# Fourier mixers: transform x times the norm's weights over channels, the token's factor at the copy out of PSUM; x in four transfers at launch

## The reference

```python
def rms_norm(x, g):
    xf = x.astype(jnp.float32)
    y = xf * lax.rsqrt(jnp.mean(xf * xf, axis=-1, keepdims=True) + EPS)
    return (y * g.astype(jnp.float32)).astype(x.dtype)

def fourier_mixer(h, w_out):
    b, s, d = h.shape
    hg = h.astype(jnp.float32).reshape(b, s, N_FOURIER_GROUPS, FOURIER_GROUP)
    f = jnp.fft.fft2(hg, axes=(1, 3), norm="ortho").real
    return f.reshape(b, s, d).astype(h.dtype) @ w_out
```

## Time and profile before

| | |
|---|---|
| runs, median (lowest to highest) | 2574.54 us (2573.38 to 2581.89), 3 runs |
| profiled execution, first to last instruction | 2575.1 us; no other time of this execution is given |
| mean granted clock of TensorE | 0.981 of full speed |
| busy: TensorE, DVE, ACT, GpSimd | 96%, 69%, 49%, 9% |
| launch to the first projection | 34.5 us |
| end of the ffn before the second Fourier mixer to its projection | 21.5 us |

### The profile page before, as it was taken

How to read it: one execution, slowest core, us unless ns; L and a number is a source line. 1 busy time by engine, 2 the same in 40 slices (tenths; PEclk the granted TensorE clock), 3 DMA queues, 4 the chain that set the end, 5 groups by cost and what they waited for, 6 DMA issues and landing times.

```text
span 2575.1 us, 54629 instructions
## 1 busy us (share of the span) xinstructions
PE 2467.8 (96%) x23198; PEld 2410.2 (94%) x23198; DVE 1778.5 (69%) x2300; ACT 1260.1 (49%) x1508; POOL 220.8 (9%) x246
## 2 busy tenths in 40 slices
PE   7999779999999899999999999999999999999998
PEld 7999669999999889989999999999999998999998
DVE  5998956665555666657666669976667667986665
ACT  5444535335666553344344346565334335675433
POOL 5000140003000100000000000600000000330000
PEclk9999879999999899999999999999999999999999
DMA  5553024555676735535545544434555554434453
GB/s 216 181 200 122 19 84 177 190 191 190 172 179 175 171 121 193 194 139 180 195 179 196 195 173 150 150 135 165 196 195 180 196 195 147 157 141 150 186 191 127
DMA packets 65839, 430.76 MB, mean 167 GB/s; under 512 B 8288, under 2 KB 11360, under 8 KB 15904
## 3 DMA queue, kind: packets, MB, share of 16 engines
q1 hardware_dynamic: 58864, 410.30, 44.0%
q0 software_dynamic: 6000, 17.46, 4.5%
q10 hardware_dynamic: 832, 0.92, 0.1%
HBM read 426.45 MB, written 1.15 MB: 166 GB/s over the span
## 4 chain that ended last, share of the span: by engine, by line
PE 85%; DVE 8%; ACT 4%; issue 2%; DMA 0%; DVEq 0%; ACTq 0%
PE psum L2018 26%; PE psum L2019 25%; PE psum L2020 25%; DVE w_lo L1332 2%; ACT w_hi L847 1%; PE psum L2063 1%; PE psum L2228 1%; PE psum L2134 1%; PE psum L2377 1%; PE psum L2365 1%; DVE h L1351 1%; DVE h_lo L1340 1%; PE psum L2355 1%; PE psum L2321 0%; PE psum L2117 0%
## 5 line engine op out<-in xcount | busy, mean ns | idle before, releaser
L2018 PE MATMUL psum<-h_hi,w_hi 128*128 128x256 f32 x4320 | 1212.7, 281 | 16.8 <-DVE h_lo L1376 9.6
L2019 PE MATMUL psum<-h_lo,w_hi 128*128 128x256 f32 x4320 | 1202.4, 278 | 0.0
L2020 PE MATMUL psum<-h_hi,w_lo 128*128 128x256 f32 x4320 | 1202.0, 278 | 0.0
L1332 DVE TENSOR_TENSOR w_lo<-raw,w_hi 128x2048 fp32r<-128x2048 f32 x387 | 888.3, 2296 | 377.7 <-ACT w_hi L847 377.5
L847 ACT ACTIVATE w_hi<-raw 128x2048 fp32r<-128x2048 f32 x387 | 741.5, 1917 | 819.9 <-PE psum L2020 819.8
L2018 PEld LDWEIGHTS psum<-h_hi,w_hi 128*128 128x128 f32 x4320 | 817.0, 189 | 26.1 <-issue 19.1
L2019 PEld LDWEIGHTS psum<-h_lo,w_hi 128*128 128x128 f32 x4320 | 816.9, 189 | 0.5 <-issue 0.5
L2020 PEld LDWEIGHTS psum<-h_hi,w_lo 128*128 128x128 f32 x4320 | 816.4, 189 | 0.0
L2018 PE MATMUL psum<-act_hi,w_hi 128*128 128x256 f32 x1536 | 425.4, 277 | 0.7 <-DVE act_lo L1895 0.7
L2020 PE MATMUL psum<-act_hi,w_lo 128*128 128x256 f32 x1536 | 424.4, 276 | 0.0
L2019 PE MATMUL psum<-act_lo,w_hi 128*128 128x256 f32 x1536 | 424.4, 276 | 0.0
(11 more groups left out here) (334 smaller groups left out, 2359.6 us busy)
## 6 DMA issues: line engine op xcount, KB each, us to landing
raw<-in_panels SPq DMA_DIRECT2D x387, 1024.0 KB, 4.8
arena<-bias_by_distance POOLq DMA_DIRECT2D x32, 384.0 KB, 6.2
x<-in_x SPq DMA_DIRECT2D x1, 1024.0 KB, 5.7
arena<-in_s_cbd POOLq DMA_DIRECT2D x4, 256.0 KB, 2.9
arena<-in_s_b SPq DMA_DIRECT2D x1, 1024.0 KB, 15.2
arena<-in_s_c SPq DMA_DIRECT2D x1, 1024.0 KB, 17.1
hidden<-in_s_cbd POOLq DMA_DIRECT2D x4, 256.0 KB, 2.9
arena<-arena POOLq DMA_DIRECT2D x32, 32.0 KB, 1.9
```

The lines of the kernel that those rows point to most:

```text
L1332: v.tensor_tensor(w_lo[:, s, :], raw[:, s, :], w_hi[:, s, :].bitcast(F32), ALU.subtract).then_inc(lo_ready, 1)
L2018: t.matmul(o, w[0], xin[0], start=start, stop=False, skip_group_check=True)
L2019: t.matmul(o, w[0], xin[1], start=False, stop=False, skip_group_check=True)
L2020: return t.matmul(o, w[1], xin[0], start=False, stop=stop, skip_group_check=True)
```

## The change

- The norm ahead of a Fourier mixer no longer makes h = x * gain * rstd. DVE multiplies x by the gain alone (`gained`), for the second mixer between its additions at the end of the ffn before. C works on that.
- The token's factor is applied by ACT as the scale of the copy of C into `dft_tok`. As tokens are on the partitions there, the factor is a column: ACT's squares go to `dft_sums` (the memory of `hidden`), TensorE multiplies each 128x128 of them with one column of ones (`sums`, 32 passes instead of 16 of 256 columns), ACT takes the root of 128x2 and DVE its reciprocal. The copy is two instructions, one for each half of the tokens. The Sqrt table is loaded ahead of the squares.
- On TensorE the order is C(0), sums of the first three pairs, C(1), the last sums, T(0).
- At launch, x comes in four transfers with a semaphore each. gains and s5.par are issued by ACT, ahead of the DFT constants. The Exp comes before the first norm. The one-hot product, its mask, and the splits of panels 0 and 1 move into the first mixer's loop, S5's reciprocal behind it. ACT splits panel 2 before S5's trigonometry and not after.
- `load_dft` for the second mixer is issued at the start of the ffn before it.

The diff, cut: left out are declarations, counts of `const_loaded` that follow from the moves, and the loops over the stages from which the launch work is taken.

```diff
@@ -318,6 +321,7 @@
         DFT_O = S // 2 - 1
         dft_ch = arena[:, 0:2 * DFT_C]
         dft_sq = arena[:, S:S + 2 * (DFT_E + 2 * DFT_O)].rearrange("p (t n) -> p t n", t=2)
+        dft_sums = hidden[:, :, :, :, :].rearrange("p a b t s -> p (a b t) s")
         dft_tok = arena[:, 5 * S:5 * S + 2 * 2 * S].rearrange("p (b t n) -> p b t n", b=2, t=2)
@@ -579,10 +583,10 @@
 
         @block.sync
         def _(sp):
-            sp.dma_start(x[:, :, :], A["x"].rearrange("(c p) t -> p c t", p=P)).then_inc(x_loaded, 16)
-            sp.dma_start(gains[:, :], A["gains"]).then_inc(const_loaded, 16)
+            for b in range(4):
+                sp.dma_start(x[:, 2 * b:2 * b + 2, :], A["x"].rearrange("(c p) t -> p c t", p=P)[:, 2 * b:2 * b + 2, :]
+                             ).then_inc(x_loaded[b], 16)
             sp.dma_start(ident[:, :], A["ident"]).then_inc(const_loaded, 16)
-            sp.dma_start(s5.par, A["s5_lam"].rearrange("p (r c) -> p r c", r=3)).then_inc(const_loaded, 16)
             for n in range(SLOTS):
                 sp.dma_start(raw[:, n, :], A["panels"][n]).then_inc(panel_loaded[n], 16)
             for dst, name in ((s5.b, "s5_b"), (s5.c, "s5_c")):
@@ -850,11 +854,27 @@
                 a.dma_start(dft_ch, A["dft_ch"]).then_inc(dft_loaded, 16)
                 a.dma_start(dft_sq, A["dft_sq"].rearrange("(t p) n -> p t n", p=P)).then_inc(dft_loaded, 16)
 
+            def squares_of_columns(st):
+
+                n = st["norm"]
+                a.wait_ge(const_set, 4)
+                a.activation(warm[:, :], eps[:, :], ACT.Sqrt)
+                for b in range(4):
+                    if st["xr"]:
+                        a.wait_ge(x_ready, st["xr"] - 3 + b)
+                    else:
+                        a.wait_ge(x_loaded[b], 16)
+                    a.activation(dft_sums[:, 2 * b:2 * b + 2], x[:, 2 * b:2 * b + 2, :], ACT.Square).then_inc(sq_ready, 1)
+                a.wait_ge(ss_ready, n + 1)
+                a.activation(rcol[:, :], bank[3][:, 0:2], ACT.Sqrt, bias=eps[:, 0:1], scale=1.0 / D).then_inc(rms_ready, 1)
+
             def norm(st):
                 n = st["norm"]
-                a.wait_ge(x_loaded, 16)
+                if st["dft"]:
+                    squares_of_columns(st)
+                    return
                 if st["late"]:
-                    a.wait_ge(const_loaded, 48)
+                    a.wait_ge(gains_loaded, 16)
                     if st["after_ffn"]:
                         a.wait_ge(panel_done, st["n0"] - 1)
                     for b in range(4):
@@ -871,8 +891,6 @@
                                  ACT.Square).then_inc(sq_ready, 1)
                 if st["late"]:
                     split(st["n0"] + 2)
-                if st["dft"] and st["xr"]:
-                    load_dft()
                 a.wait_ge(const_set, 4)
 
                 a.activation(warm[:, :], eps[:, :], ACT.Sqrt)
@@ -904,6 +922,8 @@
                         a.wait_ge(act_ready, f * FFC + c + 1 if i is None else i * 2 + f * FFC + c + 1)
                         a.activation(act_hi[:, c % 2], act[:, c % 2], ACT.Copy).then_inc(act_hi_ready, 1)
 
+                if st["next_dft"]:
+                    load_dft()
                 split(n0 + 3)
                 silu(0, n0)
                 high(0)
@@ -930,19 +950,25 @@
                     a.wait_ge(dft_full, f * KT + 2 * b + 2)
                     a.activation(h_hi[:, 2 * b:2 * b + 2], h[:, 2 * b:2 * b + 2], ACT.Copy).then_inc(dft_hi_ready, 1)
 
+                a.wait_ge(rstd_ready, st["hn"] + 1)
                 for g in range(KT):
                     a.wait_ge(dft_tok_ready, f * KT + g + 1)
-                    a.activation(dft_tok[:, g % 2, :, 0:2 * DFT_C], bank[4 + g % 2][:, :].rearrange(
-                        "p (t n) -> p t n", t=2)[:, :, 0:2 * DFT_C], ACT.Copy).then_inc(dft_tok_copied, 1)
+                    for m in range(2):
+                        ins = a.activation(dft_tok[:, g % 2, m, 0:2 * DFT_C], bank[4 + g % 2][:, m * S:m * S + 2 * DFT_C],
+                                           ACT.Copy, scale=rcol[:, m:m + 1])
+                    ins.then_inc(dft_tok_copied, 1)
                     if g:
                         even(g - 1)
                     if g >= 3 and g % 2:
                         high((g - 3) // 2)
+                    if f == 0 and g in (2, 5):
+                        split(g // 3)
                 even(KT - 1)
                 high(KT // 2 - 1)
+                split(st["n0"] + 2)
                 if f == 0 and any(q["kind"] == "s5" for q in stages):
                     s5_prepare()
-                for p in range(4):
+                for p in range(1, 4):
                     split(st["n0"] + p + 2)
 
             def s5_prepare():
@@ -1309,16 +1335,15 @@
                 for p in range(OUT_ATT, MIX_END):
                     split(n0 + p + 2)
 
+            a.dma_start(gains[:, :], A["gains"]).then_inc(gains_loaded, 16)
+            a.dma_start(s5.par, A["s5_lam"].rearrange("p (r c) -> p r c", r=3)).then_inc(const_loaded, 16)
             load_dft()
+            a.wait_ge(const_loaded, 2 * 16)
+            a.activation(s5.t[0], s5.par[:, 2], ACT.Exp).then_inc(s5_dt_ready, 1)
             todo = {"norm": norm, "final": norm, "ffn": ffn, "fourier": fourier, "s5": s5_mixer,
                     "dilated": dilated_mixer, "mix": mixer}
-            for n, st in enumerate(stages):
+            for st in stages:
                 todo[st["kind"]](st)
-                if n == 0:
-                    a.wait_ge(const_loaded, 3 * 16)
-                    a.activation(s5.t[0], s5.par[:, 2], ACT.Exp).then_inc(s5_dt_ready, 1)
-                    split(0)
-                    split(1)
 
 
         @block.vector
@@ -1341,9 +1366,28 @@
                                                  h_hi[:, c].bitcast(F32), ALU.mult, ALU.subtract)
                 ins.then_inc(h_lo_ready, 1)
 
+            def gained(st, b):
+
+                n = st["norm"]
+                if st["xr"]:
+                    v.wait_ge(x_ready, st["xr"] - 3 + b)
+                else:
+                    v.wait_ge(x_loaded[b], 16)
+                for c in (2 * b, 2 * b + 1):
+                    ins = v.tensor_scalar(h[:, c, :], x[:, c, :], gains[:, n * KT + c:n * KT + c + 1], None, ALU.mult)
+                ins.then_inc(h_ready, 1)
+
             def norm(st):
                 n = st["norm"]
-                v.wait_ge(const_loaded, 48)
+                if st["dft"]:
+                    if not st["xr"]:
+                        v.wait_ge(gains_loaded, 16)
+                        for b in range(4):
+                            gained(st, b)
+                    v.wait_ge(rms_ready, n + 1)
+                    v.reciprocal(rcol[:, :], rcol[:, :]).then_inc(rstd_ready, 1)
+                    return
+                v.wait_ge(const_loaded, 32)
                 if st["late"]:
                     v.wait_ge(sq_ready, 4 * n + 4)
                     done = 3 * (n - st["whole"])
@@ -1445,8 +1489,12 @@
                         ALU.mult, ALU.add).then_inc(x_ready, 1)
                     if b and st["next"]:
                         late_lo(st["next"], b - 1)
+                    if b and st["next_dft"]:
+                        gained(st["next_dft"], b - 1)
                 if st["next"]:
                     late_lo(st["next"], 3)
+                if st["next_dft"]:
+                    gained(st["next_dft"], 3)
                 split(n0 + 34)
 
             def add_panel(st, k, first=0):
@@ -1477,7 +1525,14 @@
                     v.tensor_tensor(half, half, odd, ALU.add).then_inc(dft_full, 1)
                     if g >= 3 and g % 2:
                         low((g - 3) // 2)
+                    if f == 0 and g == 1:
+                        v.wait_ge(e_made, 1)
+                        v.tensor_tensor(da.e, bank[0][0:NG * HEADS, :], da.mask, ALU.add).then_inc(e_made, 1)
+                    if f == 0 and g in (3, 6):
+                        split(g // 3 - 1)
                 low(KT // 2 - 1)
+                if f == 0:
+                    s5_prepare()
                 for p in range(4):
                     split(st["n0"] + p + 2)
                     add_panel(st, p)
@@ -2118,10 +2167,24 @@
                                         dft_ch, start=True, stop=True)
                     last.then_inc(dft_tok_ready, 1)
 
+                def sums(b):
+
+                    t.wait_ge(sq_ready, 4 * st["hn"] + b + 1)
+                    for c in (2 * b, 2 * b + 1):
+                        for m in range(2):
+                            last = t.matmul(bank[3][:, m:m + 1], dft_sums[:, c, m * P:(m + 1) * P], ones[:, 0:1],
+                                            start=(c + m == 0), stop=(c == KT - 1), skip_group_check=True)
+                    if b == 3:
+                        last.then_inc(ss_ready, 1)
+
                 over_channels(0)
+                for b in range(3):
+                    sums(b)
+                over_channels(1)
```

(8 more changed lines are left out.)

22 lines of the change are left out of this document (7 added, 15 removed).

## The result

The changed kernel takes 2582.47 us (median of 20 runs, 2573.86 to 2586.64), the kernel before beside it 2578.64 (20 runs). The ratio is 1.0018, 95% interval 1.0011 to 1.0025: about 4.7 us slower (3.8 between the medians), where I had forecast 3.6 faster. My 2571 started from before's first three runs, 2574.54; with the 4.1 by which before's median is higher here, 7.4 of the 11.5 that I am off belong to the change. Three single executions of 2785, 4978 and 13784 us, far above all others of their kernels, count in none of the ratios of this document. A second set on another chip gave 1.0027 (1.0017 to 1.0037). The profiled execution took 2585.02, with a span of 2583.2.

What follows compares the result with a forecast made beforehand. TensorE was taken to bound the kernel (85% of the span), so T(0)'s start counts: second mixer -2.8 and launch net -0.8 (-3.2 + 2.45) sum to -3.6, from median 2574.54 to 2571 us, range 2566 to 2578.

Steps and rivals of the forecast that it cites:

- Second mixer, -2.8: Second Fourier mixer: T(0) starts at about 1122.05 instead of 1124.83, minus 2.8 us; bounds minus 3.7 and minus 1.4.
- Rival B: Both mixers: the clock stays up through the shorter wait before T(0), giving 2568, or 2565 at best; chance 0.20.
- Constants for f = 1, nothing: Start of the ffn before the second mixer: issuing its DFT constants there costs nothing, or 0.5 if ACT has no slack.
- Launch to T(0), -3.2: Launch: ident lands at 8.8, the clock rises near 14.2, T(0) starts near 18.05, 3.2 us earlier than 21.25.
- all slow: Launch bound: every one-column pass at half clock, sums end at 19.3, T(0) at 20.4, 0.85 us earlier.
- The loop, +2.45: First mixer's loop: moved product and splits add 0.85 + 0.25 + 0.8 + 0.55 = 2.45 us; bounds 0.85 and 10.1.
- S5's trigonometry, nothing: Behind the first mixer's loop: later S5 reciprocal and trigonometry cost nothing, since nothing asks for them before the ffn.
- Rival D: Launch loop: moved work exposed whole on ACT and DVE, launch loses 6.9 against f = 1's 2.8: 2578.6; chance 0.08.
- C: Both mixers: the 32 passes neither bring nor hold full clock; launch +1.6, f = 1 -1.4: 2574.7; chance 0.22.
- Rival E: Launch: a second table load's time (1.28) between Sqrt load and squares, T(0) 0.9 later: 2571.8; chance 0.02.

Runs made afterwards that it cites:

- gap_all: gap_splits plus Exp not waiting for ident, S5 trigonometry between squares and splits, second mixer's matrices asked for later in ffn 2; 1.0004 of the kernel before.
- launch_only: The changed kernel with the second mixer's part taken back, so only launch and first mixer are changed; 1.0007 of the kernel before.
- own_wait: The changed kernel with ScalarE's Exp and GpSimd's first step no longer waiting for ident; one run, 2589.87 us beside 2578.38 for the kernel before.
- combined: The changed kernel with own_wait's edit, zero products, one-hot product and splits 0 and 1 ahead of T(0), S5 trigonometry at g = 2; 1.0016 of before.
- pe_warm: The changed kernel with 26 products of zeros on TensorE ahead of C(0); 1.0041 of the kernel before.
- streamed: The changed kernel with own_wait's edit, zeros and one-hot before C(0), trigonometry between squares and Sqrt, second mixer's matrices later; splits stay in loop; 1.0006 of before.
- gap_trig: gap_splits with the S5 trigonometry moved into the first mixer's loop at g = 2; one run, 2576.14 us beside 2578.38 for the kernel before.
- gap_splits: The changed kernel with splits 0 and 1 and the one-hot product moved out of the loop, ahead of T(0); 0.9996 of the kernel before.

## Why the prediction was wrong

**Second mixer, -2.8: right in its mechanism, and 3.2 at the place where it was forecast.** On the prediction's own reading, from the end of the ffn in the chain, T(0) came at 5.58 instead of the 6.0 forecast (8.78 before). C(0), the sums and C(1) took 4.4 (4.6 said), the passes 0.11 and less, and VectorE's split ended at 1129.83, ahead of the reciprocal at 1130.54. The gain to projection 0 is 21.86 - 19.44 = 2.4, since the lower level of the clock, which earlier covered C(0) to T(0), now begins with T(0), and takes in the first T and C of the loop. That loss behind T(0) the prediction did not have. Rival B (the clock holds) did not come: T(0) took 1.90 and the window from it stands at 0.53. In nine traces of the fourteen with this edit the stage took 50.9 to 51.1; in five it took 52.06 to 53.69, and there the lower level lasts twice as long as in the nine, in gap_all three times. The row on which B leaned, the clock's fall behind the wait of 3.43, is itself not regular: three of the four traces with the old second mixer have it, launch_only has not.

**Constants for f = 1, nothing: right.** From ffn 2's reciprocal to its last matmul it is 172.94 before and 172.95 after.

**Launch to T(0), -3.2: failed, measured +0.4** (and 0.0 in the mean of all traces). This is the step that failed, in two of its terms. Ident landed at 10.2 and not 8.8: it was issued at 2.77, behind four parts of x, and took 7.42 (I had given 9.7 as the bound). The sums so began at 12.56 and not 11.6. Taking ident out of the way gives back only half a microsecond (own_wait), since the last part of x lands just ahead of it; what x in four parts costs the prediction had put at nothing. And the clock did not rise at 14.2. This is the larger term. I had taken the rise from the 16 wide passes, 3.5 from their start, and carried it over to passes of one column; they never raised it. All 32 ran at 0.19 to 0.22, as in my bound "all slow", which gave 20.4; with the sums 1.0 later and 0.2 in small terms it is what was measured. What the runs showed in place of the rise: the passes began at the level that they found (combined 0.11 a pass, pe_warm 0.22 behind a wait of 2.12, streamed 0.21 behind 2.70); in no trace did it rise during them, and in two it fell (combined at 14.99, gap_all at 1121.38). In the changed kernel a wait of 1.26 stands ahead of the sums and one of 1.21 behind them; own_wait has only the second, and the same passes at 0.21. No run has wide sums in the new order, so how much of the late rise is the passes' and how much the waits' stays open.

**The loop, +2.45: +4.7** (18.8 before and 23.5 after, from T(0) to projection 0's last pass). Its four terms, from T(0)'s start to the next: T(3)'s wait 0.19 (0.25 said), T(6)'s 0.97 (0.8), projection 0's 0.46 (0.55), all well sized. The first was wrong by the same error: from T(0) to T(2) it is 3.1 more and not 0.85, since the product took 1.87 at the lower level, and since the clock rose at 29.05 instead of 24.02, behind T(1) instead of ahead of it, 1.2 more.

**S5's trigonometry, nothing: 1.35.** I wrote that nothing asks for it before the ffn. True, but the engine that it releases was not looked at: GpSimd starts 9.65 later, and its 128x256 instructions lie beside VectorE when the ffn's norm needs h_lo, four of which then take twice as long. gap_trig and gap_all, which bring the trigonometry forward, have a tail 1.5 and 1.3 shorter than gap_splits.

**The sum:** +0.4 + 4.3 + 0.46 + 1.35 - 2.4 = +4.1, with +3.8 between the medians and +4.7 by the ratio. Rival D has this very sum (+6.9 - 2.8 = +4.1), and that is luck: it took T(0) to start 3.2 earlier and all of the moved work to be exposed, and neither came. By mechanism the nearest was C, which had the clock right at launch (+1.6) and would have come to 2573.7 with the second mixer as it was (2574.5 + 1.6 - 2.4); ident, the product at half clock and the trigonometry are what it lacked. Rival D's mechanism, the exposed splits, is real, but at 1.6 and not 10.1. Rival E had no part: the table load at 10.49 took 1.28, the warm root began at 11.79 and the first square at 11.90, with no drain between; it goes against the drain of which the Trainium skill (ScalarE: Activation LUTs, What ACT_TABLE_LOAD costs) tells.

## What to carry to other kernels

A cheap form of an operation has to be priced at the clock that it will find: here thin passes took the place of wide ones ahead of T(0), the clock rose 5.0 later than before, and everything up to there ran at half rate. A step that is moved has to be priced at its consumers too, one engine further on: here ScalarE's trigonometry was forecast as free, and the GpSimd work that it releases was not. A transfer that is cut into parts has to be followed to its last part: it landed 3.5 later than the whole had. And when two places change, look at each in its own stage: +6.3 and about -2 are plain in the traces, while the whole's time needed some twenty runs.

## What the hardware showed unexpectedly

- TensorE streams dense passes of 128x256 at one of two paces, 0.1133 or 0.1178 from one start to the next, at the same granted clock of 1.00 and without waits, for a whole stage; five of 18 traces had one such stage, 6.5 to 6.7 us longer.
- VectorE's h_lo of 128x256 takes 0.94 to 0.97 beside a GpSimd instruction of 128x256 (31 of 31), 0.47 to 0.64 beside other work of GpSimd (81), 0.47 to 0.49 alone (32).
- One-column fp32 passes took 0.10 to 0.11 at 2.4 GHz and 0.19 to 0.22 at 1.2 GHz. None of the traces with these sums at launch has the clock rise during them; in combined it fell under them.
- The same wait of 3.43 ahead of the same passes was followed by the lower level in three executions (C(0) and C(1) 1.90 in before) and not in a fourth (1.13, launch_only).
- The landing of the same 383 KB transfer lies between 10.03 and 11.34 in the four executions of the changed launch (9.7 to 11.8 over all kernels with it); in streamed a landing at 11.35 decided the clock behind it.
